# GpSimd takes the sine product of the dilated tiles, ScalarE puts the turned maps' copies between the swapped copies, VectorE takes a head's row maxima ahead of the modulation sums

## The chip, the cores and the metric

The kernel runs on one core of one Trainium2 chip. The core has a matmul engine (TensorE, PE in the profile), three elementwise engines (VectorE = DVE, ScalarE = ACT, GpSimd = POOL) and a queue engine (SyncE = SP) that issues the transfers of the weights. Each engine works through its own list of instructions in order and waits on semaphores that the others raise. The metric is the device time of one execution in microseconds (us), lower is better.

## The reference, cut to what matters

One transformer block with a modulation, latent attention (8 heads) and dilated attention (8 heads), a gated feed-forward with a short convolution, and then two layers of another block. The change touches only the first block's attention:

```
mod = silu(c) @ w_ada + b_ada                  # 6144 columns; sh1, sc1, g1, sh2, sc2, g2
h   = rms_norm(x) * (1 + sc1) + sh1
proj = h @ w_in                                # also qd, kd, vd of the dilated attention
o_mla = causal attention over 8 heads (96 wide queries and keys, 64 wide values)
qd = rope(rms_norm(qd, g_dil_q), positions)    # 8 heads of 64: x1*cos - x2*sin, x1*sin + x2*cos
kd = rope(rms_norm(kd, g_dil_k), positions)
o_dil = dilated attention of qd, kd, vd
```

All activations are kept with features along the 128 partitions and the 512 positions along the free axis. A product of float32 precision is made of three matmuls (high and low part of each operand).

## The kernel before, in words

**Weights** come as units of 1 MB (16 blocks of 128x128) into two buffers `raw`, strictly in the order of one list (`STREAM`), by SyncE. Load v may start once the unit two places earlier is used up. A unit of weights is split by ScalarE (`split`, L1131, the high part) and then by VectorE (L1627, the low part), and TensorE multiplies with both. A unit of the modulation's matrix ("ada", a = 8 to 19 here) is not split: VectorE multiplies it by silu(c) and adds up (`ada_acc`, L1712, L1715, L1717: two instructions, then six, then one, over 128x256), and TensorE sums over the partitions with two matmuls (`ada_sums`, L479). The list around the change: z8, ada12, ada13, z10, ada14, ada15, z12, ada16, ada17, z14, ada18, ada19, z16. The four units z10 to z16 hold the columns for the dilated tiles 4 to 11.

**The loop over eight heads** h = 0 to 7 of the latent attention is where the change lies. Each head's turn makes at the same time tile z(h+2) of the dilated projection. On each engine one turn is, in order:

- TensorE: half of z(h+2) (`z_half`, L409 to L411, 12 matmuls), for even h the transposes of the last pair's output (`pair_features`, L725, waits for `otok`), the other half, the scores of head h+1 (`head_scores`, L649), the transposes of head h's first two map banks (`head_turn`, L690), the column sums of z(h+2)'s squares (`statistics`, L602, waits for ScalarE's squares), the transposes of the third map bank (L690 again, waits until ScalarE has copied the first bank out), the product with the values (`head_mix`, L707), `ada_sums(11+h)`, and for odd h the transposes of the next pair's values.
- ScalarE: for odd h `split` of the next z unit, `z_out(h+2)`, `head_turned(h)` (L1359, three copies of the transposed maps), `head_exp(h+1)`.
- VectorE: `ada_out`, `ada_acc(12+h)`, for odd h `split` of the next z unit, `head_sum(h)` (L2035), `head_top(h+1)` (L1991 with the row maximum, L1995 its negation), `sine(z, h+2)` (L1905), and for odd h `pair_otok` (L2042), for which `pair_features` waits.
- GpSimd: `rotate(z, j)`: cosine product (L2467), then the sum (L2470).

`z_out(j)` copies the tile out of PSUM bank 6 (L1289), squares it (L1273), and makes the half-swapped copy in `tmp` by four instructions of 32 rows (L1298). TensorE may overwrite bank 6 with the next tile once all four are done (`moved`). The swapped copy is multiplied by the sine and added to the tile. Tiles z(0) to z(7) go this way (z(0) and z(1) ahead of the loop), the value tiles z(8) to z(11) are only copied. `otok` of pair p needs the products of heads 2p and 2p+1; it is transposed in the next head's turn.

Of the kernel before, what the change touches and what calls it, by code (L numbers as in the profile page):

```python
# [9 lines left out]
ACT = mybir.ActivationFunctionType  # L10
# [142 lines left out]
class Signals:  # L153
# [9 lines left out]
    def inc(self, kind, *step, by=1):  # L163
        if kind not in self.sems:
            self.sems[kind] = self.ctx.enter_context(self.nc.semaphore("s_" + kind))
        self.count[kind] = self.count.get(kind, 0) + by
        if self.built:
            assert self.value[step] == (kind, self.count[kind]), (kind, step)
        else:
            assert step not in self.value, step  # L170
            self.value[step] = (kind, self.count[kind])
        return self.sems[kind], by
# [4 lines left out]
    def at(self, *step):  # L177
        if not self.built:
            return None, 0
        kind, v = self.value[step]  # L180
        return self.sems[kind], v
# [12 lines left out]
def build(nc, wstream, ada_in, x_in, pos_in, cols_in, layer_in, const_in, strip_in, bucket_in, rel_in, lru_in, y_out):  # L194
    scratch = nc.dram_tensor("bias_by_distance", (8, 640), F32, kind="Internal").ap()
    strips_dram = nc.dram_tensor("bias_strips", (8, P, S), F32, kind="Internal").ap()
    with ExitStack() as ctx:
        sig = Signals(nc, ctx)
        inc, land, at = sig.inc, sig.land, sig.at
# [34 lines left out]
        tmp = [place(f"tmp{s}", [P, S]) for s in range(4)]  # L234
        rstd = place("rstd", [P, S])
        stat = [place(f"stat{s}", [P, 16]) for s in range(4)]
        ps = ctx.enter_context(nc.psum_tensor("ps", [P, 8, S], F32))
# [13 lines left out]
        vt, zv = region("vt", 25, [P, 4, S]), region("zv", 17, [P, 4, S])  # L251
# [37 lines left out]
        TURN_GAIN = own[:, 4:6]  # L289
# [43 lines left out]
        def bank(b, m=P, n=S, lo=0):  # L333
            return ps[lo:lo + m, b, 0:n]
# [789 lines left out]
        def act_program(act):  # L1124
            def split(u):
                act.wait_ge(*at("raw", AT[UNITS[u]]))
                if u == N_UP:
                    act.wait_ge(*at("pair_mix", 7))
                elif u >= 2:
                    act.wait_ge(*at("unit", u - 2))  # L1130
                act.activation(hi_of(u)[:], raw[AT[UNITS[u]] % 2][:], ACT.Copy).then_inc(*inc("hi", "hi", u))  # L1131
# [135 lines left out]
            def squares(t, rows, b):  # L1267
                n = NORMED.index(t)
                if n >= 2:
                    act.wait_ge(*at("stat", NORMED[n - 2]))  # L1270
                else:
                    act.wait_ge(*at("lat_sum", "kv", n))
                act.activation(sq[n % 2][0:rows, :], bank(b, rows), ACT.Square).then_inc(*inc("tile", "tile", t))  # L1273
# [11 lines left out]
            def z_out(j, b):  # L1285
                u = UNIT["z", 6 + j - j % 2]
                act.wait_ge(*(at("unit", u) if j % 2 else at("z_mm", j)))
                if j < 8:
                    act.activation((zq if j < 4 else zk)[:, j % 4, :], bank(b), ACT.Copy)  # L1289
                    squares(("z", j), P, b)  # L1290

                    n = TURNED.index(("z", j))
                    act.wait_ge(*at("roped", TURNED[n - 2]))
                    if j == 0:
                        act.wait_ge(*at("turn_gain", 3))
                    for r in range(4):
                        w, to = slice(32 * r, 32 * r + 32), 32 * (r ^ 1)
                        ins = act.activation(tmp[n % 2][to:to + 32, :], ps[w, b, :], ACT.Copy, scale=TURN_GAIN[w, j // 4:j // 4 + 1])  # L1298
                    ins.then_inc(*inc("moved", "moved", ("z", j)))
                else:  # L1300
                    act.activation(zv[:, j - 8, :], bank(b), ACT.Copy).then_inc(*inc("tile", "tile", ("z", j)))

            def head_seed(kind, b, n, out, bias):

# [23 lines left out]
                    split(7)  # L1328
            head_seed("kv", 2, 10, r_kv, KV_EPS)
            z_out(0, 6)  # L1330
            split(8)
            z_out(1, 6)


            def head_exp(h):
# [13 lines left out]
            def head_turned(h):  # L1349
                if h == 9:  # L1350
                    act.wait_ge(*at("roped", ("z", 7)))
                elif h >= 10:
                    act.wait_ge(*at("pair_mix", h // 2 - 1))
                elif h >= 1:
                    act.wait_ge(*at("mix", h - 1))
                out = PT if h < 8 else PT_pair[h % 2]
                for b, w, to in ((0, 512, 0), (1, 512, 512), (2, 256, 1024)):
                    act.wait_ge(*at("turn", h, b))
                    act.activation(out[:, to:to + w], ps[:, (3, 4, 3)[b], 0:w], ACT.Copy).then_inc(*inc("turned", "turned", h, b))  # L1359
# [15 lines left out]
            for h in range(8):  # L1375
                if h % 2 == 0 and h:
                    pair_out(h // 2 - 1)
                if h % 2:
                    split(9 + h // 2)
                z_out(h + 2, 6)  # L1380
                head_turned(h)
                if h == 5:
                    head_exp(h + 1)
                    head_seed("z", 7, 16, r_z, EPS[0:16])
                elif h < 7:
                    head_exp(h + 1)
                if h % 2 and h < 7:
                    head_values(h + 1)
# [234 lines left out]
        def dve_program(dve):  # L1623
# [77 lines left out]
            def ada_acc(a):  # L1701
                k = BY_DVE.index(a)
                part = acc(a)[:].rearrange("p (e n) -> p e n", e=2)
                dve.wait_ge(*at("raw", AT["ada", a]))
                dve.wait_ge(*at("silu_c"))
                if k >= 2:
                    dve.wait_ge(*at("ada_mm", BY_DVE[k - 2]))
                for kt in range(DT):
                    w = raw[AT["ada", a] % 2][:, 2 * kt:2 * kt + 2, :].rearrange("p b n -> p (b n)")
                    c, y = SILU_C[:, kt:kt + 1], part[:, kt % 2, :]  # L1710
                    if kt < 2:
                        dve.tensor_scalar(y, w, c, None, ALU.mult).then_inc(*inc("ada_part", "ada_part", a, kt))  # L1712
                    else:
                        dve.wait_ge(*at("ada_part", a, kt - 2))
                        dve.scalar_tensor_tensor(y, w, c, y, ALU.mult, ALU.add).then_inc(*inc("ada_part", "ada_part", a, kt))  # L1715
                dve.wait_ge(*at("ada_part", a, DT - 1))
                dve.tensor_tensor(part[:, 0, :], part[:, 0, :], part[:, 1, :], ALU.add).then_inc(*inc("ada_part", "ada_sum", a))  # L1717
# [181 lines left out]
            def sine(t):  # L1899

                _, rows, _, _, sin = source(t)
                n = TURNED.index(t)
                if t[0] == "z":
                    dve.wait_ge(*at("moved", t))
                    dve.tensor_tensor(tmp[n % 2][:], tmp[n % 2][:], sin[:], ALU.mult).then_inc(*inc("sin", "sin", t))  # L1905
                    return
                b = 6 + n % 2
                dve.wait_ge(*at("turned_t", t))
                dve.wait_ge(*(at("roped", TURNED[n - 2]) if n >= 2 else at("table", 1)))
                dve.tensor_tensor(tmp[n % 2][0:rows, :], bank(b, rows), sin[0:rows, :], ALU.mult).then_inc(*inc("sin", "sin", t))  # L1910
# [55 lines left out]
            head(("qn", 3), 0)  # L1966
            head(("qp", 0), 1)
            head(("qp", 1), 0)
            sine(("z", 0))
            dve.wait_ge(*at("scale", "rms"))  # L1970
            for i in range(4):
                dve.wait_ge(*at("tile", ("v", i)))
# [75 lines left out]
                dve.tensor_tensor(lo[:] if p < 4 else lo, bank(5), (hi[:] if p < 4 else hi).bitcast(F32), ALU.subtract).then_inc(*inc("out_lo", "out_lo", p))  # L2048

            head_top(0)  # L2050
            sine(("z", 1))
            ada_acc(11)
            for h in range(8):
                if h % 2 == 0 and h:
                    pair_out(h // 2 - 1)
                if h:
                    ada_out(10 + h, 3, 0)
                if h == 6:
                    head_root("z", 7, 16, r_z, EPS[0:16])
                ada_acc(12 + h)  # L2060
                if h % 2:
                    split(9 + h // 2)
                head_sum(h)
                if h < 7:
                    head_top(h + 1)
                if h < 6:
                    sine(("z", h + 2))
                else:
                    head(("z", 4 * (h - 6)), 7)
                if h % 2:  # L2070
                    pair_otok(h // 2)
# [356 lines left out]
        def pool_program(pool):  # L2428
# [31 lines left out]


            def rotate(t):
                tile, rows, _, cos, _ = source(t)
                n = TURNED.index(t)
                pool.wait_ge(*(at("moved", t) if t[0] == "z" else at("turned_t", t)))
                pool.wait_ge(*at("cosines", 0 if t[0] == "z" else 1))
                pool.tensor_tensor(tile, tile, cos[0:rows, :], ALU.mult).then_inc(*inc("rotated", "cos_t", t))  # L2467
                pool.wait_ge(*at("sin", t))
                pool.wait_ge(*at("cos_t", t))
                pool.tensor_tensor(tile, tile, tmp[n % 2][0:rows, :], ALU.add).then_inc(*inc("rotated", "roped", t))  # L2470
# [275 lines left out]
```

## Time and profile before

| | us |
|---|---|
| median of 3 runs | 2607.41 (2603.93 to 2608.01) |
| the profiled execution, its time | 2607.48 |
| its span | 2606.2 |
| PE busy | 2562.6 (98%) |
| DVE busy | 1242.7 (48%) |
| ACT busy | 951.4 (37%) |
| POOL busy | 168.6 (6%) |
| mean granted TensorE clock | 0.995 |

An engine's busy time is the sum over its instructions; the granted clock is the share of TensorE's full clock that the chip let through. The stretch that the change touches lies between about 150 and 290 us. The time of the profiled execution is 1.3 us more than its span.

### The profile page before, as it was taken

Reading aid. Unit: us, or ns where it says so; the run is one execution under the profiler, and the core shown is the slowest. Engines: PE = TensorE matmul, PEld = TensorE weight load, DVE = VectorE, ACT = ScalarE, POOL = GpSimd, SP = SyncE. Lnnn points to the kernel's source line nnn. Section 1 sums busy time; section 2 is a strip of 40 time slices with the busy share of each in tenths; the row PEclk is TensorE's granted clock in tenths of the full one; section 3 lists DMA queues with packets and bytes.
Section 4 is the critical chain, followed back from the end, with each engine's and each line's share of the span. In section 5 each row is a group of like instructions: output and inputs, shape, how many; then the busy total and the mean of one; then the engine's idle time right before and its main releaser. Section 6 shows DMA issues by size and latency. Waiting matters only on the chain.

```text
span 2606.2 us, 27657 instructions
## 1 busy us (share of the span) xinstructions
PE 2562.6 (98%) x11527; PEld 2053.2 (79%) x11527; DVE 1242.7 (48%) x1775; ACT 951.4 (37%) x1288; POOL 168.6 (6%) x168
## 2 busy tenths in 40 slices
PE   7999999999999999999999999999999999999998
PEld 4557678888888888877788888888888777888886
DVE  5675665665343333356643333333343466533333
ACT  4456454443232222245532222322222355422221
POOL 0111000000001110000001110011100000011100
PEclk9999999999999999999999999999999999999999
DMA  6432212332322222332222223222223322222231
GB/s 248 151 114 99 85 65 97 113 130 97 112 99 97 97 97 97 113 108 71 81 97 97 97 97 114 97 97 97 97 97 113 105 73 81 97 97 97 97 113 65
DMA packets 41390, 267.20 MB, mean 103 GB/s; under 512 B 5449, under 2 KB 5833, under 8 KB 11698
## 3 DMA queue, kind: packets, MB, share of 16 engines
q1 hardware_dynamic: 37440, 256.92, 28.6%
q0 software_dynamic: 2576, 7.10, 0.8%
q8 instruction: 91, 1.49, 0.2%
q10 hardware_dynamic: 1250, 1.42, 0.2%
q14 instruction: 33, 0.27, 0.0%
HBM read 262.78 MB, written 4.21 MB: 102 GB/s over the span
## 4 chain that ended last, share of the span: by engine, by line
PE 94%; DVE 3%; ACT 1%; issue 1%; DMA 0%; SPq 0%; DVEq 0%; ACTq 0%
PE ps L409 29%; PE ps L411 28%; PE ps L410 28%; PE ps L959 1%; PE ps L707 1%; ACT tmp L1298 1%; PE ps L690 1%; PE ps L993 1%; PE ps L579 0%; DVE wlo L1627 0%; PE ps L663 0%; DMA early<-ada_in 0%; PE ps L980 0%; PE ps L581 0%; PE ps L580 0%
## 5 line engine op out<-in xcount | busy, mean ns | idle before, releaser
L1627 DVE TENSOR_TENSOR wlo<-raw,whi 128x2048 fp32r<-128x2048 f32 x213 | 488.1, 2291 | 1066.9 <-ACT whi L1131 1066.7
L409 PE MATMUL ps<-ahi,whi 128*128 128x512 f32 x2272 | 897.4, 395 | 4.9 <-DVE alo L1747 4.9
L411 PE MATMUL ps<-alo,whi 128*128 128x512 f32 x2272 | 886.5, 390 | 0.0
L410 PE MATMUL ps<-ahi,wlo 128*128 128x512 f32 x2272 | 886.4, 390 | 0.0
L1131 ACT ACTIVATE whi<-raw 128x2048 fp32r<-128x2048 f32 x213 | 407.8, 1914 | 884.3 <-PE ps L411 882.9
L409 PEld LDWEIGHTS ps<-ahi,whi 128*128 128x128 f32 x2272 | 427.9, 188 | 102.0 <-issue 8.5
L411 PEld LDWEIGHTS ps<-alo,whi 128*128 128x128 f32 x2272 | 427.6, 188 | 90.5
L410 PEld LDWEIGHTS ps<-ahi,wlo 128*128 128x128 f32 x2272 | 427.8, 188 | 88.8 <-issue 2.4
L409 PE MATMUL ps<-hhi,whi 128*128 128x512 f32 x1008 | 393.2, 390 | 3.4 <-DVE hhi L2281 3.4
L410 PE MATMUL ps<-hhi,wlo 128*128 128x512 f32 x1008 | 392.2, 389 | 0.0
L411 PE MATMUL ps<-hlo,whi 128*128 128x512 f32 x880 | 342.4, 389 | 0.0
L409 PEld LDWEIGHTS ps<-hhi,whi 128*128 128x128 f32 x1008 | 189.2, 188 | 44.7 <-DVE hhi L2281 4.7
L410 PEld LDWEIGHTS ps<-hhi,wlo 128*128 128x128 f32 x1008 | 189.3, 188 | 39.2
L2500 POOL TENSOR_TENSOR tmp<-tmp,rstd 128x512 f32<-128x512 f32 x88 | 111.8, 1292 | 1556.6 <-ACT tmp L1449 1556.6
L411 PEld LDWEIGHTS ps<-hlo,whi 128*128 128x128 f32 x880 | 165.2, 188 | 34.1
L1456 ACT ACTIVATE hhi<-tmp 128x512 fp32r<-128x512 f32 x110 | 67.7, 633 | 176.9 <-DVE tmp L2177 130.1
L1449 ACT ACTIVATE tmp<-tmp 128x512 f32<-128x512 f32 x110 | 68.1, 633 | 165.1 <-DVE tmp L2172 133.2
L2183 DVE TENSOR_TENSOR hlo<-tmp,hhi 128x512 fp32r<-128x512 f32 x110 | 71.1, 688 | 5.4
L2141 DVE SCALAR_TENSOR_TENSOR tmp<-ps,cols,tmp 128x511 f32<-128x511 f32 (+1 forms) x88 | 59.7, 740 | 0.0
L2172 DVE TENSOR_TENSOR tmp<-ps,rstd 128x512 f32<-128x512 f32 x88 | 56.4, 681 | 0.0
L2177 DVE TENSOR_TENSOR tmp<-tmp,ps 128x512 f32<-128x512 f32 x88 | 56.2, 681 | 0.0
L2209 DVE TENSOR_TENSOR z<-ps,rstd 128x512 f32<-128x512 f32 x44 | 29.9, 686 | 49.5 <-PE ps L411 49.2
(379 smaller groups left out, 1725.9 us busy)
## 6 DMA issues: line engine op xcount, KB each, us to landing
raw<-wstream SPq DMA_DIRECT2D x221, 1024.0 KB, 4.8
raw<-wstream SPq DMA_DIRECT2D x24, 512.0 KB, 5.0
early<-ada_in SPq DMA_DIRECT2D x8, 1024.0 KB, 21.8
strip<-bias_strips POOLq DMA_DIRECT2D x16, 256.0 KB, 3.8
x<-x_in SPq DMA_DIRECT2D x2, 1024.0 KB, 6.9
bias_strips<-bias_by_distance POOLq DMA_DIRECT2D x1, 2048.0 KB, 16.7
y_out<-x SPq DMA_DIRECT2D x3, 512.0 KB, 2.7
bd<-lru_in ACTq DMA_DIRECT2D x2, 256.0 KB, 12.2
```

Of the source, the lines that this page charges most:

```text
L409: pe.matmul(out, wh, rhi, start=start, stop=False)
L410: pe.matmul(out, wl, rhi, start=False, stop=False)
L411: return pe.matmul(out, wh, rlo, start=False, stop=stop)
L1131: act.activation(hi_of(u)[:], raw[AT[UNITS[u]] % 2][:], ACT.Copy).then_inc(*inc("hi", "hi", u))
L1449: act.activation(tmp[m][:], tmp[m][:], ACT.Silu).then_inc(*inc("silu", "silu", f, i, m))
L1456: act.activation(hhi[:, 2 * i + m, :], tmp[m][:], ACT.Copy).then_inc(*inc("h_hi", "h_hi", f, 2 * i + m))
L1627: dve.tensor_tensor(lo_of(u)[:], raw[r][:], hi_of(u)[:].bitcast(F32), ALU.subtract).then_inc(*inc("lo_dve", "lo", u))
L2141: dve.scalar_tensor_tensor(tmp[b][:, d:], bank(b, n=S - d), col(w, j), tmp[b][:, d:], ALU.mult, ALU.add)\
L2172: dve.tensor_tensor(tmp[m][:], bank(m), rstd[:], ALU.mult).then_inc(*inc("gate_out", "gate_out", f, i, m))
L2177: dve.tensor_tensor(tmp[m][:], tmp[m][:], bank(2 + m), ALU.mult)\
L2183: dve.tensor_tensor(hlo[:, 2 * i + m, :], tmp[m][:], hhi[:, 2 * i + m, :].bitcast(F32), ALU.subtract)\
L2500: pool.tensor_tensor(tmp[m][:], tmp[m][:], rstd[:], ALU.mult).then_inc(*inc("silu_r", "silu_r", f, i, m))
```

## The change

ScalarE's swapped copies are taken out of `z_out` into `z_move(j, b, head)`, which makes two of the four. In the loop they stand on both sides of `head_turned(h)`; for z(0) and z(1) both calls follow `z_out` at once. `sine` of the dilated tiles goes from VectorE's list to `rotate` on GpSimd, between the cosine product and the sum. In VectorE's loop `ada_acc(12+h)` goes from ahead of `split`, `head_sum` and `head_top` to behind them, still ahead of `pair_otok`.

```diff
@@ act_program, z_out
                     squares(("z", j), P, b)
-
-                    n = TURNED.index(("z", j))
+                else:
+                    act.activation(zv[:, j - 8, :], bank(b), ACT.Copy).then_inc(*inc("tile", "tile", ("z", j)))
+
+            def z_move(j, b, head):
+
+                n = TURNED.index(("z", j))
+                if head == 0:
                     act.wait_ge(*at("roped", TURNED[n - 2]))
                     if j == 0:
                         act.wait_ge(*at("turn_gain", 3))
-                    for r in range(4):
-                        w, to = slice(32 * r, 32 * r + 32), 32 * (r ^ 1)
-                        ins = act.activation(tmp[n % 2][to:to + 32, :], ps[w, b, :], ACT.Copy, scale=TURN_GAIN[w, j // 4:j // 4 + 1])
+                for r in (2 * head, 2 * head + 1):
+                    w, to = slice(32 * r, 32 * r + 32), 32 * (r ^ 1)
+                    ins = act.activation(tmp[n % 2][to:to + 32, :], ps[w, b, :], ACT.Copy, scale=TURN_GAIN[w, j // 4:j // 4 + 1])
+                if head:
                     ins.then_inc(*inc("moved", "moved", ("z", j)))
@@ act_program, the loop over h
                 z_out(h + 2, 6)
+                if h < 6:
+                    z_move(h + 2, 6, 0)
                 head_turned(h)
+                if h < 6:
+                    z_move(h + 2, 6, 1)
@@ dve_program
                 n = TURNED.index(t)
-                if t[0] == "z":
-                    dve.wait_ge(*at("moved", t))
-                    dve.tensor_tensor(tmp[n % 2][:], tmp[n % 2][:], sin[:], ALU.mult).then_inc(*inc("sin", "sin", t))
-                    return
...
-            sine(("z", 0))
...
-            sine(("z", 1))
@@ dve_program, the loop over h
-                ada_acc(12 + h)
                 if h % 2:
                     split(9 + h // 2)
                 head_sum(h)
                 if h < 7:
                     head_top(h + 1)
-                if h < 6:
-                    sine(("z", h + 2))
-                else:
+                ada_acc(12 + h)
+                if h >= 6:
                     head(("z", 4 * (h - 6)), 7)
                 if h % 2:
                     pair_otok(h // 2)
@@ pool_program, rotate
                 pool.tensor_tensor(tile, tile, cos[0:rows, :], ALU.mult).then_inc(*inc("rotated", "cos_t", t))
+                if t[0] == "z":
+                    pool.tensor_tensor(tmp[n % 2][:], tmp[n % 2][:], sin[:], ALU.mult).then_inc(*inc("rotated", "sin", t))
                 pool.wait_ge(*at("sin", t))
```

## Rows read from the trace of the kernel before

**Rows 1.** Busy time by stretch: start:end, its length, busy of each engine, clock, DMA
```profile
180.00:200.00 20.00, 18.11 (x91) 14.95 (x91) 14.81 (x40) 12.24 (x27) 3.95 (x3) 0.85 0.44 159
...
220.00:240.00 20.00, 18.66 (x111) 14.28 (x109) 12.02 (x33) 14.34 (x30) 4.67 (x4) 1.00 0.33 121
```

**Rows 2.** TensorE's waits, 160 to 262 us: total us, times, longest
```profile
PE ps L690 <- ACT PT L1359: 5.2, 6, 1.9
PE ps L633 <- DVE kt L1932: 0.4, 1, 0.4
```

**Rows 3.** Busy time by stretch, the stretch of the low clock (behind POOL's column)
```profile
194.00:200.80 6.80, 6.80 (x29) 6.32 (x29) 0.94 (x2) 2.79 (x9) 1.27 (x1) 0.51 0.25 105
```

**Rows 4.** TensorE in order of time: start, us, engine line, [idle before <- releaser]
```profile
193.05 0.41 PE L690 MATMUL ps<-const,E 128*128 128x128 f32 x2 [1.89 <-ACT PT L1359]
...
202.43 0.60 PE L725 MATMUL ps<-const,otok 128*128 128x128 f32 x4
...
205.63 2.32 PE L649 MATMUL ps<-kt,qt 96*128 96x512 f32 x8
207.78 1.04 PE L690 MATMUL ps<-const,E 128*128 128x128 f32 x8
...
210.46 0.41 PE L690 MATMUL ps<-const,E 128*128 128x128 f32 x2 [0.67 <-ACT PT L1359]
...
223.75 0.41 PE L690 MATMUL ps<-const,E 128*128 128x128 f32 x2 [0.67 <-ACT PT L1359]
...
229.91 0.60 PE L725 MATMUL ps<-const,otok 128*128 128x128 f32 x4
```

**Rows 5.** ScalarE in order of time, heads 1 and 2
```profile
186.62 1.91 ACT L1131 ACTIVATE whi<-raw 128x2048 fp32r<-128x2048 f32 x1
...
188.92 0.59 ACT L1273 ACTIVATE sq<-ps 128x512 f32<-128x512 f32 x1
...
206.94 2.75 ACT L1298 ACTIVATE tmp<-ps,own 32x512 f32<-32x512 f32 x4
209.71 1.57 ACT L1359 ACTIVATE PT<-ps 128x512 f32<-128x512 f32 x3
```

**Rows 6.** VectorE in order of time, heads 2 and 3
```profile
204.38 0.61 DVE L1712 TENSOR_SCALAR tmp<-raw,small 128x256 f32<-128x256 f32 x2
204.90 2.46 DVE L1715 SCALAR_TENSOR_TENSOR tmp<-raw,small,tmp 128x256 f32<-128x256 f32 x6
207.39 0.42 DVE L1717 TENSOR_TENSOR tmp<-tmp 128x256 f32<-128x256 f32 x1
...
207.99 0.69 DVE L1991 CUSTOM_DVE_ANT_0 E<-ps,strip_row 128x512 f32<-128x512 f32 x1
...
209.75 0.17 DVE L1995 TENSOR_SCALAR stat<-stat 128x4 f32<-128x4 f32 x1
209.83 1.77 DVE L1905 TENSOR_TENSOR tmp<-tmp,sin_dil 128x512 f32<-128x512 f32 x1
...
217.02 2.29 DVE L1627 TENSOR_TENSOR wlo<-raw,whi 128x2048 fp32r<-128x2048 f32 x1
...
226.44 0.69 DVE L2042 TENSOR_TENSOR otok<-ps,sel 128x512 f32<-128x512 f32 x1 [1.55 <-PE ps L707]
```

**Rows 7.** GpSimd in order of time, beside VectorE's L1905 above and L1715 below
```profile
124.01 1.41 POOL L2470 TENSOR_TENSOR qp<-qp,tmp 128x512 f32<-128x512 f32 x1
...
209.77 1.29 POOL L2467 TENSOR_TENSOR zk<-zk,cos_dk 128x512 f32<-128x512 f32 x1 [14.16 <-ACT tmp L1298]
```

**Rows 8.** VectorE in order of time, `ada_acc(10)` beside GpSimd's sum of `qp`
```profile
123.16 1.12 DVE L1712 TENSOR_SCALAR tmp<-raw,small 128x256 f32<-128x256 f32 x2
124.20 3.48 DVE L1715 SCALAR_TENSOR_TENSOR tmp<-raw,small,tmp 128x256 f32<-128x256 f32 x6
```

**Rows 9.** SyncE's issue of load z10, and all of the loads' times to landing
```profile
181.92 0.33 SPq L2547 DMA_DIRECT2D raw<-wstream  x1
...
DMA to landing us min/median/max: 4.5/4.8/6.8
```

More of the change, by code:

```diff
@@ L1295, in z_out @@
                         act.wait_ge(*at("turn_gain", 3))
-                    for r in range(4):
-                        w, to = slice(32 * r, 32 * r + 32), 32 * (r ^ 1)
-                        ins = act.activation(tmp[n % 2][to:to + 32, :], ps[w, b, :], ACT.Copy, scale=TURN_GAIN[w, j // 4:j // 4 + 1])
+                for r in (2 * head, 2 * head + 1):
+                    w, to = slice(32 * r, 32 * r + 32), 32 * (r ^ 1)
+                    ins = act.activation(tmp[n % 2][to:to + 32, :], ps[w, b, :], ACT.Copy, scale=TURN_GAIN[w, j // 4:j // 4 + 1])
+                if head:
                     ins.then_inc(*inc("moved", "moved", ("z", j)))
-                else:
-                    act.activation(zv[:, j - 8, :], bank(b), ACT.Copy).then_inc(*inc("tile", "tile", ("z", j)))
             def head_seed(kind, b, n, out, bias):
@@ L1330, in act_program @@
             z_out(0, 6)
+            z_move(0, 6, 0)
+            z_move(0, 6, 1)
             split(8)
             z_out(1, 6)
+            z_move(1, 6, 0)
+            z_move(1, 6, 1)
             def head_exp(h):
@@ L2065, in dve_program @@
                     head_top(h + 1)
-                if h < 6:
-                    sine(("z", h + 2))
-                else:
+                ada_acc(12 + h)
+                if h >= 6:
                     head(("z", 4 * (h - 6)), 7)
@@ L2462, in rotate @@
             def rotate(t):
-                tile, rows, _, cos, _ = source(t)
+                tile, rows, _, cos, sin = source(t)
                 n = TURNED.index(t)
```

## The prediction

> **What bounds the kernel now.** First the page: TensorE is busy for 98% of the span, so only its idle time and its clock can be won, and any new idle time is paid in full. Then busy time by stretch: of the 20 us from 180 it is idle 1.9 at a mean clock of 0.85, of the 20 us from 220 it is idle 1.3 at full clock [rows 1]. Its waits say for whom: six times, 5.2 us in all, the transposes of the third map bank (L690) wait until ScalarE has copied the first bank out (L1359), and once 0.4 us for the head of a key tile [rows 2]. In order of time one of the six is 1.89 us, in head 1, the other five 0.67 each [rows 4]. Behind the long one the granted clock falls to 0.51, which is the 1.2 GHz level, for 6.8 us [rows 3]; behind the waits of 0.67 it stays at 1.00 [rows 1]. What that costs: from the second transposes of head 1 to the features L725 it takes 202.43 - 193.05 = 9.38 us [rows 4]; the same work two heads on, at full clock, 229.91 - 223.75 = 6.16, so 3.2 us. All that could be won is thus 5.2 + 0.4 + 3.2 = 8.8 us.
>
> **Part 1, ScalarE's order.** The four swapped copies take 2.75 us and stand ahead of the three map copies [rows 5]. With two of them behind, the first bank comes free 1.38 us earlier: the five waits of 0.67 go (3.4), and 1.38 of the 1.89. What is late next: the statistics end where the wait now begins, so nothing more. `moved` comes behind the third map copy: that starts some 0.4 us after the third transposes start, takes 0.4, and two copies 1.38, so bank 6 is free 2.2 us after the third transposes start. TensorE wants it behind head_mix and the sums, 0.25 + 2.24 + 0.42 = 2.9 later. Hidden by head_mix, with 0.7 spare; with no cover it would cost up to 1.4 a head. Gain if nothing else moved: 4.8 us.
>
> **Part 2, the sine product on GpSimd.** VectorE loses eight instructions of 0.6 to 1.77 us [rows 6], which were behind the maxima and on nobody's path, but for z(0), ahead of the value and key tiles: those are 0.6 us earlier and the 0.4 wait goes. GpSimd gets eight of 1.28. Its chain per tile is 3.85 us instead of 3.2, and nobody needs the tile before the swapped copy two heads on, or the norm in head 6. GpSimd's own queue has its next piece 13 us later. The instruction by itself is hidden. What isn't is the collision: VectorE's sine beside GpSimd's cosine product took 1.77 us, from 209.83 to 211.60; GpSimd's ended at 211.06, and 0.54 are left for the work itself [rows 6, 7]. VectorE stood still for the whole of the other's product. In `ada_acc` the same: alone its six L1715 take 2.46 [rows 6], beside GpSimd's sum 3.48 [rows 8]. And GpSimd's sum, asked for while VectorE's L1712 ran, took 1.41 instead of 1.28 [rows 7]: it gets its turn behind one instruction of VectorE's. So back-to-back pieces of the two alternate, and each of GpSimd's costs an `ada_acc` beside it 1.27 us.
>
> The Trainium skill, "SBUF — State Buffer", section "Who interferes with whom", says so too: whoever of the two starts first holds the shared port pair for its whole instruction and the other is fully blocked. By that rule the sum below stands; were the pair shared by bandwidth, as one might think, the terms of 1.27 would be about half, and the sum some 4 us less. The rows above agree with the lock.
>
> The maxima L1991 read PSUM and aren't held up; their negation L1995 and every instruction of `ada_acc` are.
>
> **Part 3, `ada_acc` behind the maxima.** Before, `ada_acc` filled VectorE's wait for the scores and was done when they came (at 207.73, the maxima start at 207.99) [rows 6]. Behind them it meets GpSimd's three products of that head, which start with `moved`, 2.6 us or less after the maxima. Two things wait for it: `pair_otok`, next on VectorE's list in odd heads, for which L725 waits; and SyncE, whose load z10 went out at 181.92 [rows 9], the moment `ada_acc(12)` had read its last block. Loads z12 and z14 hang the same way on `ada_acc(14)` and `ada_acc(16)`, and for them wait ScalarE's split, which stands ahead of `z_out`, then the statistics.
>
> Heads 0 and 1: the key tiles give 0.35, the wait in head 0 0.67. `ada_acc(11)` ends its reads at 172.9 (173.4 before), ada12 lands at 177.7, `ada_acc(12)` needs 3.0 alone, and two products of GpSimd (from 179.9) fall into it: reads done at 183.2, not 181.9. Landing 4.8 later [rows 9], split at 188.1, not 186.62 [rows 5]; 1.9 for the split, 1.1 for copy and squares (189.51 less 186.62 and 1.91, and a handoff), statistics at 191.2, two swapped copies, and L690 at 193.1, as before (193.05). VectorE: split to 192.3, maxima to 194.2, `ada_acc(13)` 3.35 + 3 x 1.27 = 7.2 to 201.4, otok 0.6, features at 202.1. Before 202.43. Should the clock fall here again, TensorE gets there at 202.6. Sum of the first pair: -0.4 to +0.2, I take +0.2.
>
> Heads 2 and 3, from features to features: 27.48 before [rows 4], with 1.34 of waiting. Now the chain is: features 0.36, half a tile 2.73, scores 2.16 [rows 4], start of the maxima 0.2, maxima and negation 1.85, reads of `ada_acc(14)` 3.0 [rows 6] with one product 1.27 (it starts 2.6 behind the maxima), landing 4.8, split on ScalarE 1.9, on VectorE 2.2, reciprocal 0.1, maxima 1.85, `ada_acc(15)` 3.35 with three products 3.8, otok 0.6, handoffs 0.2. Sum 30.4, that is +2.9 us. TensorE then idles 0.7 ahead of the statistics, 1.0 at L690 and 2.6 ahead of L725. Heads 4 and 5 the same, +2.9. Heads 6 and 7 have no products; the load z16 behind `ada_acc(18)` makes +0.4.
>
> The clock: in heads 3 and 5 the idle 1.7 stands in one place, about as the 1.89 that was followed by the low clock. A fall there costs 3.2, of which 2.6 vanish in the wait ahead of L725: +0.6 each, 1.2.
>
> **Sum**: 0.2 + 2 x 2.9 + 0.4 + 1.2 = +7.6. Behind 290 us TensorE has only single waits up to 0.5 and takes the delay over whole. The profiled execution took 2607.48 (span 2606.2, 1.3 around it), at the median of the runs, 2607.41: 2615.0 us.
>
> **Bounds of the unknown.** How many products fall into a chained `ada_acc`: one fewer in each of the three odd heads makes 3 x 1.27 = 3.8 us less; one more ahead of each load 2.5 more. The landing at 4.5 or 5.2 makes -1.3 to +3. The clock: none to 6.6.
>
> **Rivals.** *Gain as meant.* If VectorE got ahead of a waiting GpSimd whenever it had work, `ada_acc` would keep its 3.35. Then features come 1.2 us behind otok and all is hidden: -4.8 - 0.35 - 3.2 (a wait of 0.5 is left, and the clock stays up) = -8.3, less some 1 of leftover waits: 2600. It decides with the first product inside `ada_acc(15)`, whose 1.27 is the whole slack. For: TensorE's waits are real. Against: GpSimd's 1.41. *Some collisions only*: GpSimd's pieces run mostly into VectorE's PSUM work, or the landing is short: between -3 and +4, about 2608. *The clock falls behind each wait ahead of L725* instead: 2.6 us idle, then 4.9 us of half a tile and scores on the chain at 1.2 GHz: +3.3 in heads 4 and 6 rather than 0.6: 2615.0 - 1.2 + 6.6 = 2620.4. For: 2.6 is longer than 1.89. Against: an earlier fall, at L690, eats that wait.
>
> **How the numbers follow.** About 0.2% (5.2 us) is what a measurement of this kernel tells from no change. Forecast 0.50 (2611 to 2619), clock rival 0.12, some collisions 0.22, gain 0.16. The forecast's lower end lies within 5.2 of before, so slower by more than 0.2% gets 0.60, within 0.25, faster 0.15. The range goes from 2604, which leaves out the gain rival, to 2622.
>
> **What would show it.** In the profile after: L1715 beside GpSimd's L2467 and the new product at over 5 us for six where GpSimd runs beside it; L725 idle before it with VectorE's otok as releaser, 2 to 3 us, three times at most; L602 waiting for ScalarE's squares in heads 1, 3, 5; the five waits of 0.67 at L690 gone in even heads; SyncE's load z12 six us later than 207.38. Wrong if L725 has no wait, or if six L1715 stay at 2.5 us while GpSimd runs.

## The result, and the profile after

| | before | after |
|---|---|---|
| median | 2607.74 us (20 runs) | 2611.84 us (20 runs) |
| ratio to before, 95% interval | | 1.0021 (1.0015 to 1.0028) |
| the profiled execution, its time / span | 2607.48 / 2606.2 | 2611.39 / 2610.1 |
| mean granted TensorE clock | 0.995 | 0.996 |
| POOL busy | 168.6 | 182.1 |
| spread of the runs | 2603.93 to 2612.34 | 2606.17 to 2619.24 |

The change makes the kernel slower: by 0.21% or 5.5 us by the ratio (3.9 to 7.3 by its interval), by 4.1 between the two medians. The forecast was +7.6.

TensorE's waits between 160 and 292 us (us in all, times, longest); they sum to 12.0 us, before to 5.6. In place of six waits at L690 [rows 2] stand waits for three things; the fourth row (the output projection waits for ScalarE's copy of a value tile) is one that the prediction didn't have, and the fifth was to go:

```profile
PE ps L725 <- DVE otok L2049: 5.4, 3, 1.8
PE ps L690 <- ACT PT L1367: 3.5, 4, 1.1
PE ps L602 <- ACT sq L1273: 1.9, 3, 1.1
PE ps L409 <- ACT zv L1292: 0.8, 1, 0.8
PE ps L633 <- DVE kt L1940: 0.4, 1, 0.4
```

In order of time, heads 1 to 3. In the even head 2 the wait at L690 is gone, as it should; the odd heads 1 and 3 wait at L602 and L690, and the features of the pair wait in the next head [answers to rows 4]:

```profile
188.84 1.03 PE L602 MATMUL ps<-sq,sel 128*16 128x512 f32 x2 [1.13 <-ACT sq L1273]
190.94 0.41 PE L690 MATMUL ps<-const,E 128*128 128x128 f32 x2 [1.06 <-ACT PT L1367]
...
199.05 0.66 PE L725 MATMUL ps<-const,otok 128*128 128x128 f32 x4 [1.78 <-DVE otok L2049]
...
206.39 0.44 PE L690 MATMUL ps<-const,E 128*128 128x128 f32 x2
...
218.56 1.03 PE L602 MATMUL ps<-sq,sel 128*16 128x512 f32 x2 [0.48 <-ACT sq L1273]
220.66 0.41 PE L690 MATMUL ps<-const,E 128*128 128x128 f32 x2 [1.06 <-ACT PT L1367]
...
228.78 0.66 PE L725 MATMUL ps<-const,otok 128*128 128x128 f32 x4 [1.84 <-DVE otok L2049]
```

VectorE in heads 2 and 3 [answers to rows 6]. The six instructions of the sums take 3.49 and 5.55 us, where they took 2.46. In head 3 the first three take 0.48 each as before, the last three 1.50 to 1.51. Otok comes at the end of them:

```profile
206.54 0.61 DVE L1724 TENSOR_SCALAR tmp<-raw,small 128x256 f32<-128x256 f32 x2
207.07 3.49 DVE L1727 SCALAR_TENSOR_TENSOR tmp<-raw,small,tmp 128x256 f32<-128x256 f32 x6
...
217.43 2.29 DVE L1639 TENSOR_TENSOR wlo<-raw,whi 128x2048 fp32r<-128x2048 f32 x1 [5.37 <-ACT whi L1131]
...
222.11 5.55 DVE L1727 SCALAR_TENSOR_TENSOR tmp<-raw,small,tmp 128x256 f32<-128x256 f32 x6
...
228.04 0.68 DVE L2049 TENSOR_TENSOR otok<-ps,sel 128x512 f32<-128x512 f32 x1
```

GpSimd beside them [answers to rows 7], the cosine product of head 2, then cosine product, sine product and sum of head 3. Each takes longer than 1.28 too, as if it had to let one of VectorE's pass first:

```profile
208.72 1.56 POOL L2471 TENSOR_TENSOR zk<-zk,cos_dk 128x512 f32<-128x512 f32 x1 [11.07 <-ACT tmp L1303]
...
222.96 1.56 POOL L2471 TENSOR_TENSOR zk<-zk,cos_dk 128x512 f32<-128x512 f32 x1 [9.82 <-ACT tmp L1303]
224.48 1.48 POOL L2473 TENSOR_TENSOR tmp<-tmp,sin_dil 128x512 f32<-128x512 f32 x1
226.04 1.34 POOL L2476 TENSOR_TENSOR zk<-zk,tmp 128x512 f32<-128x512 f32 x1
```

And the transfer that hangs on them: SyncE issues load z12 at 210.59, when L1727 is done (207.07 + 3.49 = 210.56). ScalarE has been idle for 4.53 us when it lands, splits at 215.49, and only behind that, at 217.43, copies the tile whose last matmul TensorE ended at 215.05:

```profile
210.59 0.33 SPq L2553 DMA_DIRECT2D raw<-wstream  x1
```
```profile
215.49 1.91 ACT L1131 ACTIVATE whi<-raw 128x2048 fp32r<-128x2048 f32 x1 [4.53 <-DMA raw<-wstream]
217.43 0.60 ACT L1289 ACTIVATE zk<-ps 128x512 f32<-128x512 f32 x1
217.92 0.59 ACT L1273 ACTIVATE sq<-ps 128x512 f32<-128x512 f32 x1
```

The clock, by stretch (behind POOL's column). The stretch that had 0.85 [rows 1] has 1.00 in this execution, with more idle time than before, and another one fell:

```profile
180.00:200.00 20.00, 16.03 (x87) 12.28 (x86) 12.89 (x24) 10.94 (x24) 7.05 (x5) 1.00 0.21 66
...
290.00:300.00 10.00, 10.00 (x37) 6.79 (x38) 5.51 (x16) 3.66 (x11) 0.00 (x0) 0.83 0.39 105
```

**Where the 3.9 us between the two spans are.** TensorE comes to tile 2's first half at 166.38, 1.78 earlier than before; 1.80 of it is there already ahead of the first place that the change touches, so the change didn't make it. (From 20 to 40 us the mean granted clock is 0.91 in this execution and was 0.83 before.) From there to the features of pair 3 it takes 120.48 us, before 117.34: +3.14 (and before had the low clock in it, 3.2). Behind them 2.62 are lost within 8 us, 0.8 by the wait for `zv`, the rest with the clock at 290. By pairs, the first from tile 2's first half to its features, then from features to features: -1.60, +2.25, +2.10, +0.39.

### The profile page after: what moved, and what is told of

The parts are those of the page before. It is cut to its first block, busy times and chain, and to the rows that moved or that the text cites. A ratio compares the mean times of both kernels' runs of the same rounds, so it can differ in the third digit from the quotient of the medians.

```text
span 2610.1 us, 27657 instructions
## 1 busy us (share of the span) xinstructions
PE 2559.1 (98%) x11527; PEld 2049.4 (79%) x11527; DVE 1247.1 (48%) x1767; ACT 951.4 (36%) x1288; POOL 182.1 (7%) x176
## 4 chain that ended last, share of the span: by engine, by line
PE 91%; DVE 5%; DMA 1%; issue 1%; ACT 1%; SPq 0%; DVEq 0%
PE ps L409 28%; PE ps L411 28%; PE ps L410 28%; DVE tmp L1727 1%; DMA raw<-wstream 1%; PE ps L959 1%; PE ps L993 1%; PE ps L579 0%; DVE E L1998 0%; PE ps L649 0%; PE ps L980 0%; DMA early<-ada_in 0%; PE ps L581 0%; PE ps L580 0%; DVE wlo L1639 0%
## 5 line engine op out<-in xcount | busy, mean ns | idle before, releaser
L409 PE MATMUL ps<-ahi,whi 128*128 128x512 f32 x2272 | 897.2, 395 | 6.6 <-DVE alo L1759 5.8
L409 PEld LDWEIGHTS ps<-ahi,whi 128*128 128x128 f32 x2272 | 427.5, 188 | 103.9 <-issue 9.5
L409 PE MATMUL ps<-hhi,whi 128*128 128x512 f32 x1008 | 393.2, 390 | 3.4 <-DVE hhi L2285 3.4
L409 PEld LDWEIGHTS ps<-hhi,whi 128*128 128x128 f32 x1008 | 189.2, 188 | 44.8 <-DVE hhi L2285 4.7
```

The lines of the kernel that those rows point to most:

```text
L409: pe.matmul(out, wh, rhi, start=start, stop=False)
```

## The experiments

Two theories at first. **A**: GpSimd's products stop VectorE's sums; otok and the loads wait for the sums, and TensorE for both. **B**: the order of the sums alone makes the loads late, GpSimd or not. Then, within A, **L** (the loads cost most) against **O** (otok costs most), and **C**, that the clock decides by chance. All times are medians, each with its ratio to the before that ran beside it and the 95% interval; before was at 2607.73 for E1 to E4, 2607.56 for E5 to E8 and 2607.64 for E9 to E12. The changed kernel's 2611.84 was measured apart from these groups, so a difference to it is less sure than one to before.

**E1, ScalarE's order alone**: the change without its other two parts.

> Only ScalarE's order is changed (two swapped copies on each side of the map copies); the sine product stays on VectorE and the modulation sums stay ahead of the maxima. Theory A (GpSimd's products stop VectorE's modulation sums, and otok and the loads wait for these): here nothing is chained that way, so the waits of 0.67 us at L690 and most of the 1.9 us go: -3.5 us, and -3.2 more where the clock no longer falls in head 1, 2600 to 2604. Theory B (the order of the sums alone makes the loads late, collisions or not): the same, 2600 to 2604. Theory C (the clock's falls decide, and the loop is a matter of chance): anything from -8 to 0, with another clock.

2602.05 us, 0.9979 (0.9970 to 0.9988). One wait of 0.7 is left at L690, of 5.2 us before. The part that was meant to win wins, 5.7 us.

**E2, with the sine product on GpSimd.** As the changed kernel, but

```diff
             for h in range(8):
                 ...
+                ada_acc(12 + h)
                 if h % 2:
                     split(9 + h // 2)
                 head_sum(h)
                 if h < 7:
                     head_top(h + 1)
-                ada_acc(12 + h)
```

> ScalarE's order and the sine product on GpSimd, but the modulation sums ahead of split and maxima as before. Theory A: two of GpSimd's products still fall into the sums of the next head, but the sums end 2 us before the scores come, so the collision is hidden: within 1 us of the kernel with ScalarE's order alone, 2600 to 2604; L725 doesn't wait. Theory B: the same. If collisions cost wherever they are: +2 us or more against that kernel.

2600.74, 0.9974 (0.9964 to 0.9985), and once more (E11) 2600.97, 0.9976 (0.9967 to 0.9984). GpSimd's work costs nothing that can be seen here, though two of the sums still meet it (L1727 3.57). This kernel is the changed one but for one line's place: that place costs 11 us.

> The kernel with ScalarE's order and GpSimd's sine product, sums ahead of the maxima, once more beside the two others on the same chip. All theories: 2600 to 2602.

**E3, ScalarE's order and the sums behind the maxima**, the sine product on VectorE behind the sums.

> ScalarE's order and the modulation sums behind the maxima, the sine product on VectorE as before, behind the sums. Theory A: the sums meet one product of GpSimd instead of three; the slack of 1.2 us ahead of L725 about takes it, so -1 to -4 against before, 2603 to 2606, L725 waits under 0.5 us. Theory B: the loads z10, z12, z14 leave late anyway: +2 to +4, 2610 to 2612.

2608.47, 1.0008 (0.9999 to 1.0018): 6.4 more than E1. I had expected 2603 to 2606 by A. The profile shows one collision in each head from head 1 to 5 (L1727 3.48 to 3.50), with GpSimd's cosine product, L725 waiting 0.35 twice, and L602 and L690 waiting 3.9 in all. So it doesn't part A from B: one collision at the right place may have been enough to make the load late, and so may the order. E7 was made for that.

**E4, otok ahead of the sums in odd heads.**

```diff
-                ada_acc(12 + h)
+                if h % 2 == 0:
+                    ada_acc(12 + h)
                 if h >= 6:
                     head(("z", 4 * (h - 6)), 7)
                 if h % 2:
                     pair_otok(h // 2)
+                    ada_acc(12 + h)
```

> The changed kernel with otok ahead of the modulation sums in odd heads. Theory A, otok's part: the three waits at L725 (5.4 us in all in the profile of after) go, and the rest stays: -4 to -5 against after, 2607 to 2608. Theory B: the loads behind the even heads' sums are what costs, otok's wait only hides behind them: within 1 us of after, 2611.

2608.81, 1.0014 (1.0003 to 1.0024). The three waits at L725 are gone, yet only 3.0 us are back of the 5.4, less than the 4 to 5 that I had expected: L409 now waits 2.8 for `zv`, in place of 0.8, since the load for the output projection leaves behind the sums of head 7, and these behind otok.

**E5 and E6, the sums ahead in even, or in odd heads only.**

```diff
+                if h % 2 == 0:        # E6: == 1
+                    ada_acc(12 + h)
                 if h % 2:
                     split(9 + h // 2)
                 ...
-                ada_acc(12 + h)
+                if h % 2 == 1:        # E6: == 0
+                    ada_acc(12 + h)
```

> The changed kernel, but in even heads the modulation sums stand ahead of the maxima again (they free the buffer for the loads z10, z12, z14, z16); in odd heads behind, as changed. Theory L (the late loads cost most): waits at L602 and L690 in heads 3 and 5 gone, the waits at L725 smaller, 1.2 us each: 2603 to 2606. Theory O (the sums ahead of otok cost most): L725 still waits 1.8 us three times and the time stays within 2 us of the changed kernel's 2611.8.

> The mirror image: the sums ahead of the maxima in odd heads only, behind them in even heads. Theory O: no wait at L725, and the load for the output projection leaves in time: 2604 to 2606. Theory L: the loads z10 to z16 are still late, L602 and L690 wait 1 to 2 us in heads 1, 3 and 5: 2608 to 2611.

E5: 2602.19, 0.9975 (0.9966 to 0.9985). E6: 2609.69, 1.0003 (0.9992 to 1.0015). L holds: 9.7 of the 11 us come back with the even heads' sums alone, those that free the buffer for z10 to z16, and I had expected less, 2603 to 2606. L725 waits in neither, so otok is late only where two things meet: a late split with the maxima behind it, and sums between these and otok. The two gains therefore overlap and can't be added up. E6 has 6.2 us less of waits than the changed kernel and is only 2.1 faster; its profiled execution had a low clock from 220 to 260 (0.81 and 0.83), so a part of its gain is hidden by the clock. In E5 the sums of head 1 still take 5.53 for six, and it costs nothing. TensorE's waits from 140 us on, E5 and then E6:

```profile
PE ps L690 <- ACT PT L1367: 1.1, 1, 1.1
PE ps L633 <- DVE kt L1940: 0.4, 1, 0.4
PE ps L630 <- DVE qt L1940: 0.4, 1, 0.4
PE ps L602 <- ACT sq L1273: 0.3, 1, 0.3
```
```profile
PE ps L690 <- ACT PT L1367: 3.4, 4, 1.1
PE ps L602 <- ACT sq L1273: 2.0, 3, 1.0
PE ps L633 <- DVE kt L1940: 0.4, 1, 0.4
PE ps L630 <- DVE qt L1940: 0.4, 1, 0.4
```

**E7, GpSimd's products on one column.** In `rotate`, `w = slice(0, 1 if t[0] == "z" else S)` on all operands; the rotation of the other columns is left out.

> The changed kernel with GpSimd's three instructions per dilated tile on one column instead of 512 (the rotation of the dilated tiles is left out). Theory A (collisions stretch the sums, the order by itself is harmless): the six L1727 take 2.5 us everywhere, L725 doesn't wait, 2599 to 2602. Theory B (the order by itself): 2606 to 2608, as with the sine product on VectorE.

2601.77, 0.9979 (0.9969 to 0.9989). The order is that of the changed kernel, the six L1727 take 2.46 in every head, and 10 us are back. B falls as the cause of the loss. The order alone isn't free: L690 still waits 2.3 us in four heads and L409 0.7, where E1 keeps 0.7 in one.

**E8, the sine product on GpSimd alone**, on the kernel before.

> The kernel before with only the sine product moved to GpSimd. Theories A and B alike: the collisions fall into sums that end before the scores come, the six waits at L690 are unchanged, 0.35 us are won at the key tiles: 0 to -1 against before. If GpSimd's products cost wherever they are: +2 or more.

2610.51, 1.0008 (1.0000 to 1.0017), where I had expected no loss or a gain of up to 1; by the interval it is barely told from before. In head 0 the sums wait for their transfer until the products have begun; six instructions take 5.49, the load z10 leaves at 183.73 (181.92 before), and head 1 waits 1.0 at L602 and 2.5 at L690. VectorE, then TensorE:

```profile
178.21 5.49 DVE L1715 SCALAR_TENSOR_TENSOR tmp<-raw,small,tmp 128x256 f32<-128x256 f32 x6
```
```profile
191.43 1.03 PE L602 MATMUL ps<-sq,sel 128*16 128x512 f32 x2 [0.97 <-ACT sq L1273]
194.92 0.66 PE L690 MATMUL ps<-const,E 128*128 128x128 f32 x2 [2.46 <-ACT PT L1359]
```

**E9, GpSimd held back.** The changed kernel with all its work, and one wait more:

```diff
                 pool.wait_ge(*at("cosines", 0 if t[0] == "z" else 1))
+                if t[0] == "z" and t[1] >= 2:
+                    pool.wait_ge(*at("ada_sum", 10 + t[1]))
                 pool.tensor_tensor(tile, tile, cos[0:rows, :], ALU.mult)...
```

> The changed kernel with one wait more: GpSimd starts a tile's three products only when VectorE has finished that head's modulation sums. All the work and the order of the lists stay. Theory A (collisions stretch the sums; loads and otok wait for them): the six L1727 take 2.5 us everywhere, the waits at L725 go and those at L602 nearly, 2600 to 2603, as with one-column products. Theory B (the one-column kernel won because there was less work, or GpSimd's products cost in another way): 2607 or more.

2599.26, 0.9973 (0.9962 to 0.9983). The products now begin behind the sums, each takes 1.3 again, and the load z12 leaves when L1727's 2.46 are over. GpSimd, VectorE and SyncE of E9:

```profile
207.25 1.30 POOL L2473 TENSOR_TENSOR zk<-zk,cos_dk 128x512 f32<-128x512 f32 x1 [8.77 <-DVE tmp L1729]
208.51 1.29 POOL L2475 TENSOR_TENSOR tmp<-tmp,sin_dil 128x512 f32<-128x512 f32 x1
```
```profile
204.16 2.46 DVE L1727 SCALAR_TENSOR_TENSOR tmp<-raw,small,tmp 128x256 f32<-128x256 f32 x6
...
218.12 2.46 DVE L1727 SCALAR_TENSOR_TENSOR tmp<-raw,small,tmp 128x256 f32<-128x256 f32 x6
...
220.96 0.68 DVE L2049 TENSOR_TENSOR otok<-ps,sel 128x512 f32<-128x512 f32 x1
```
```profile
206.65 0.33 SPq L2555 DMA_DIRECT2D raw<-wstream  x1
```

This is the cleanest of the runs: nothing is left out, no list is reordered, and it is 12.6 us faster than the changed kernel. Some 9 of these are waits: from 160 us on TensorE's sum to 3.3 instead of 12.0. Executions with the same mean clock say so too: the median span is 9.3 less at 0.996 (2 runs and 4) and 9.4 less at 0.997 (5 and 2). The rest goes with a higher mean clock. The 2.0 us that L690 and the 0.9 that L409 still wait are the order's own price, as in E7.

**E10, the best version**: E2, but in head 0 the sums stand behind the maxima, and only tile 2's products are held back.

> ScalarE's order and GpSimd's sine product, modulation sums ahead of the maxima from head 1 on, in head 0 behind them (there the sums wait for their transfer anyway), and GpSimd holds the products of tile 2 back until the sums of head 0 are done. Theory A: the load z10 leaves 1 us earlier than in the changed kernel and the map's exponentials no longer stand ahead of its split, so the waits in head 1 (1.6 us in the kernel with GpSimd and ScalarE changed) fall below 1: 2599 to 2601, the fastest so far. If the wait in head 1 is set by something else: as that kernel, 2600.7.

2597.78, 0.9967 (0.9955 to 0.9979): 9.9 us under before by the medians, 8.6 by the ratio, and below the 2599 to 2601 that I had expected; its mean clock was 0.997, that of before 0.995. In head 1 one wait of 0.73 is left at L690, none at L602. It is faster than before beyond doubt; that it is faster than E9 or E2 the intervals don't show.

**E12, the changed kernel again.**

> The changed kernel once more, on the same chip. All theories: 2610 to 2613, 4 to 6 us above before. If the clock's falls are a matter of chance, the profile shows them at other places of the loop than the first one (which had one, at 290 us), and the runs spread over 10 us and more in line with their mean clock.

2616.07, 1.0039 (1.0025 to 1.0052), five runs at a mean clock of 0.992, more than the 2610 to 2613 expected. The waits of its profiled execution are those of the first one (L725 5.4, L690 3.4, L602 2.5), so what is new is the clock; see below. Beside E9 and E11, which ran on the same chip, it is 16.8 and 15.1 us slower, more than the 12.6 and 11 above.

## Why the prediction was right or wrong

*What bounds*: right. What the runs gained or lost shows in TensorE's waits and in its clock; behind 300 us the two traces go at the same pace (3.98 apart at 300, 3.9 at the end).

*Part 1*: right. E1 won 5.7 us, where 4.8 and a chance on the clock were put; with the sums in place five of the six waits at L690 went, 4.5 us, and TensorE never waited for `moved`.

*Part 2, the collision*: the mechanism was right, its size not. Each product was put at 1.27, its whole length. It costs 1.03: 3.49 - 2.46 with one, 5.55 - 2.46 = 3 x 1.03 with three. The prediction's own rows had that number, 3.48 - 2.46 = 1.02 [rows 6, 8], and used the other. The 0.35 at the key tiles didn't come: L633 still waits 0.4, and TensorE's lead over before is 1.80 ahead of the place and 1.78 behind it. A collision that the prediction left out takes it back: VectorE's split there takes 3.08 us beside GpSimd's sum, 2.29 before. The Trainium skill ("SBUF — State Buffer", "Who interferes with whom") has the shared port pair as an exclusive lock, and for VectorE's two-port modes it says that the loser is fully blocked for the whole instruction. The runs bear the lock out in kind; by them a VectorE instruction with two inputs in SBUF loses 1.03 us to a product of 1.28.

*Part 3*: the chain is as it was written, link by link. SyncE's load z12 was to leave six us later. It leaves 3.2 later in the trace, but this execution is 3.4 ahead there: counted from the features ahead of it, it is 6.6 later (11.54 behind them, before 4.95). First pair: forecast -0.4 to +0.2, measured -1.6. One product fell into the reads of `ada_acc(12)`, not two (L1727 3.49), and the clock didn't fall there: the waits in this pair are 3.97 us against 2.56, but before also lost its 3.2 to the low clock here. Second and third pair: +2.9 each, measured +2.25 and +2.10; four products too large by 0.24 make 1.0 in a pair, more than the whole difference of 0.65 and 0.8. What the prediction had as two separate ends of the chain, the late load and the late otok, aren't separate: E5 shows that with the load in time otok's wait goes too, E6 that it goes as well with the odd heads' sums ahead, E4 that curing otok alone brings 3 us.

*Fourth pair*: +0.4, measured +0.39. What stands behind it was not seen, and it is the step of the chain that failed: the load of the output projection hangs on `ada_acc(19)` in head 7, ScalarE's split of it stands ahead of the copy of tile 10, and L409 waits 0.8. The prediction followed the loads z10 to z16 and not the next one on the same list. No product of GpSimd runs there, and L409 waits 0.7 and 0.9 in E7 and E9 too: this one is the order's doing.

*The clock*: wrong as a rule. The prediction read from one execution that a wait of 1.9 us brings the clock down and 0.67 doesn't, and put 1.2 us on falls in heads 3 and 5. None came: the clock stays at 1.00 through waits of 1.78, 1.84 and 1.83 at L725, and falls behind one of 0.80.

*The rival "gain as meant"* names the point from which it decides, and E7 and E9 are it: without the collisions the same order gives 2602 and 2599, where 2600 was worked out. With them it gives 2611.8.

The sum: 7.6 less 1.8 (first pair), 1.45 (second and third) and 1.2 (the clock) is 3.15, which is the loop's +3.14 told by its terms. The 2.62 behind it that were missed make 5.8, against 5.5 by the ratio. That these two agree, and that the forecast of 7.6 came this near, is partly luck: terms that were too large (1.27 a product, the clock, the second product in the first pair) stand against one that was missing, and 1.8 of the 2.62 is a fall of the clock in this one execution. The two profiled spans differ by 3.9 only because the execution after was 1.8 ahead when it came to the change.

## What to carry to other kernels

When work is moved to GpSimd, look at what VectorE does in SBUF at the time it will run, and at what hangs on that: here three products of 1.3 us a tile cost nothing beside slack and 11 us beside the sums that free a transfer's buffer. If the moved work isn't urgent, hold it back with one wait on the other engine's urgent work; that was worth 12.6 us, 9 of them in waits. Instructions that release a buffer of an ordered stream belong as early as their data allows, and the next entries of the stream have to be followed too.

## What the runs showed of the hardware

Where VectorE's and GpSimd's queues both read SBUF they seem to alternate one for one: GpSimd's 1.28 us product takes 1.56, 1.48 and 1.34, and three of VectorE's six instructions in a row grow from 0.48 to 1.50, 1.03 for each product. VectorE's maxima, which read PSUM, take 0.69 beside a product (at 165.11) as elsewhere.

The length of a wait doesn't settle whether the granted clock falls to its lower level, 1.2 GHz. The changed kernel, once more (E12), by stretch: it fell in the stretch from 160 (0.50 from 165 to 167.5), where two waits of 0.4 us are all that there is from 140 on, and stayed at 1.00 from 190 through waits of 1.64, 1.07 and 1.80. The first execution of the same kernel fell at 290 instead, behind a wait of 0.80, and before at 194, behind 1.89.

```profile
160.00:170.00 10.00, 9.61 (x20) 3.47 (x19) 6.87 (x17) 3.80 (x6) 3.75 (x3) 0.66 0.01 2
190.00:200.00 10.00, 7.29 (x51) 5.80 (x50) 8.00 (x18) 9.72 (x19) 2.50 (x2) 1.00 0.00 1
200.00:210.00 10.00, 8.20 (x40) 5.88 (x39) 5.15 (x10) 4.00 (x8) 1.83 (x2) 1.00 0.55 210
```

The runs spread with it: the 20 of the changed kernel go from a span of 2604.9 at a mean clock of 0.997 to 2617.9 at 0.991, of the 78 of before beside the experiments 74 lie at 0.994 to 0.996. At the same mean clock of 0.995 the median span is 2610.7 after (5 runs) and 2606.5 before (36), 4.2 apart; at 0.996 they are 6.4 apart (4 and 26 runs), at 0.993 4.0 (2 and 4), at 0.994 1.7 (1 and 12). So most of the 5.5 us doesn't come from the clock; how much does, these few runs don't settle. Whether more idle time makes a fall likelier was not tested by itself; the mean clock over all runs of a kernel was 0.994 or 0.995 in those with many waits (after, E3, E4, E6, E8; 0.992 in E12), 0.996 to 0.997 in those with few (E1, E2, E5, E7, E9, E10, E11), and 0.995 in before. That fits a link, but it isn't a test of one.
